# Gate and up products of four feed-forwards as seven block products each, in a two-block transformer kernel

## The reference, cut to what matters

```
x = x + 0.5 * swiglu(rms_norm(x, ffn_norm_g[l, 0]), ffn_w_gate[l, 0], ffn_w_up[l, 0], ffn_w_down[l, 0])
x = x + mixer(rms_norm(x, mix_norm_g[l]))
x = x + 0.5 * swiglu(rms_norm(x, ffn_norm_g[l, 1]), ffn_w_gate[l, 1], ffn_w_up[l, 1], ffn_w_down[l, 1])

swiglu(h, wg, wu, wd) = (silu(h @ wg) * (h @ wu)) @ wd      # wg, wu: 1024 x 2816, wd: 2816 x 1024
```

## Time and profile before

| | us |
|---|---|
| median of 3 runs | 3767.45 (3766.74 to 3774.5) |
| profiled execution, span from its first to its last instruction | 3773.9 |
| PE busy | 3591.6 (95%) |
| DVE, ACT, POOL busy | 1361.0, 1280.9, 1416.5 (36%, 34%, 38%) |

### The profile page before, as it was taken

One profiled execution on the slowest core, in us unless ns is written; L12 is line 12 of the kernel. 1 busy time (PEld: TensorE's weight loads), 2 busy tenths in 40 slices (PEclk: granted clock), 3 DMA queues, 4 the chain that ended last, 5 costly groups with the idle time before them and its releaser, 6 DMA issues. The chain is left out here.

```text
span 3773.9 us, 50732 instructions
## 1 busy us (share of the span) xinstructions
PE 3591.6 (95%) x18352; PEld 2848.7 (75%) x18352; DVE 1361.0 (36%) x1928; ACT 1280.9 (34%) x2014; POOL 1416.5 (38%) x756
## 2 busy tenths in 40 slices
PE   7999999999999999999999998999998997879998
PEld 6888776688887888666688886888886874648886
DVE  4233645542325223645542336111115104561112
ACT  4222435542224223435542224212123234243223
POOL 4444333344444444333344442223232430024443
PEclk8999999999999999999999999999998998889999
DMA  4332443233323333333233332222212321013331
GB/s 133 96 99 84 99 119 113 85 90 98 97 84 101 96 99 89 100 113 107 85 95 100 95 99 63 64 64 61 66 52 61 89 77 52 1 45 93 96 95 61
DMA packets 569026, 322.34 MB, mean 85 GB/s; under 512 B 30266, under 2 KB 563360, under 8 KB 568480
## 3 DMA queue, kind: packets, MB, share of 16 engines
q1 hardware_dynamic: 568864, 320.22, 29.1%
HBM read 318.08 MB, written 2.10 MB: 85 GB/s over the span
## 5 line engine op out<-in xcount | busy, mean ns | idle before, releaser
L874 POOL TENSOR_TENSOR w_lo<-w_raw,w_hi 128x1024 fp32r<-128x1024 f32 x516 | 1273.5, 2468 | 2109.4 <-ACT w_hi L919 2109.4
L919 ACT ACTIVATE w_hi<-w_raw 128x1024 fp32r<-128x1024 f32 x516 | 546.8, 1060 | 1800.7 <-PE psum L2163 1685.8
L2163 PE MATMUL psum<-xg_hi,w_hi 128*128 128x512 f32 x1456 | 572.7, 393 | 12.2 <-DVE xg_lo L1485 10.4
L2163 PE MATMUL psum<-xg_hi,w_lo 128*128 128x512 f32 x1456 | 568.2, 390 | 0.0
L2163 PE MATMUL psum<-xg_lo,w_hi 128*128 128x512 f32 x1408 | 549.5, 390 | 0.0
L2163 PE MATMUL psum<-h_hi,w_hi 128*128 128x512 f32 x1248 | 504.3, 404 | 30.7 <-DVE h_ctx_lo L1534 21.6
L2163 PE MATMUL psum<-h_lo,w_hi 128*128 128x512 f32 x1248 | 491.1, 394 | 0.0
L2163 PE MATMUL psum<-h_hi,w_lo 128*128 128x512 f32 x1248 | 491.1, 393 | 0.0
L2163 PE MATMUL psum<-a_hi,w_hi 128*128 128x512 f32 x1232 | 433.0, 375 | 4.9 <-DVE a_lo L1602 4.2
L2163 PE MATMUL psum<-a_lo,w_hi 128*128 128x512 f32 x1232 | 432.7, 374 | 0.0
L2163 PE MATMUL psum<-a_hi,w_lo 128*128 128x512 f32 x1232 | 432.3, 374 | 0.0
(11 more groups left out here) (454 smaller groups left out, 4399.7 us busy)
## 6 DMA issues: line engine op xcount, KB each, us to landing
w_raw<-ffn_w SPq DMA_DIRECT2D x120, 512.0 KB, 3.8
w_raw<-ffn_w_gate SPq DMA_DIRECT2D x88, 512.0 KB, 3.8
w_raw<-ffn_w_up SPq DMA_DIRECT2D x88, 512.0 KB, 3.8
ada_raw<-ada_w SPq DMA_DIRECT2D x72, 512.0 KB, 4.5
w_raw<-ffn_w_down SPq DMA_DIRECT2D x64, 512.0 KB, 4.1
w_raw<-w_in SPq DMA_DIRECT2D x60, 512.0 KB, 3.8
w_raw<-ffn_w_down SPq DMA_DIRECT2D x32, 384.0 KB, 3.4
w_raw<-w_out SPq DMA_DIRECT2D x24, 512.0 KB, 4.0
```

The costliest lines, as they stand in the source:

```text
L874: nc.gpsimd.tensor_tensor(w_lo[:, i, :], w_raw[:, i, :], w_hi[:, i, :].bitcast(F32), ALU.subtract).then_inc(lo_ready, 1)
L919: nc.scalar.activation(w_hi[:, pos, :], w_raw[:, pos, :], ACT.Copy).then_inc(hi_ready, 1)
L2163: last = nc.tensor.matmul(dst, w[:, pos, k * P:(k + 1) * P], rhs[g][r](k0 + k), start=k == 0 and m == 0, stop=k == nk - 1 and m == 2)
```

## The change

**The unit.** Gate and up of the four feed-forwards are no longer computed tile by tile. A *unit* is the gate (r = 0) or the up (r = 1) product for a pair of tiles, so 256 hidden features, 1024 inputs and 512 tokens. Weights and activations are cut into 2 x 2 blocks: hidden features by halves of the inputs (4 chunks each), halves of the inputs by halves of the tokens (256 each). The four blocks of the result come out of 7 block products instead of 8, by a scheme of the Strassen and Winograd kind. Each block product is 4 chunks x 3 passes = 12 matmuls of 256 tokens, so a unit has 84 matmuls of 256 where it had 48 of 512. There are 22 units in a feed-forward. PE does the products in the order 0, 2, 3, 1, 4, 6, 5. Products 0, 3, 4 and 5 accumulate into one bank (`chain`), and partial results are taken out of it between them.

**What feeds it.** The weights need 3 sums of 512 columns and a fourth one later (`set_sums_of`, `set_last_sum`), on DVE. The sums' rounded copies and rests come from ACT (`set_high`, `set_last_high`) and DVE (`sums_low`, `set_last_low`), and POOL makes two rests of 1024 per unit (`set_low`), as many as before. From a part's second pair on, two of the sums lie in PSUM, where ACT first copies a half slot (`copy_second`); a part's first pair has them in SBUF. The activations need 4 such sums, made once per feed-forward at its entry, chunk by chunk (`b_low` on DVE, `b_high` on ACT) in place of `xg_low` and `xg_high`.

**What follows it.** ACT copies three partial results per unit out of PSUM (`part_copy`), and DVE adds three and scales (`joined`). Silu, `a_hi` and `a_lo` are done once per pair on 1024 columns.

**Around it.** The loop over the two layers is written out. After F4 nothing is made for a next feed-forward (7 of `xg_high` and `xg_low` go), the load of `ctx_rows` starts later, and a Silu of the second block's conditioning has moved into the mixer. Counters of the second block are merged with those of the first.

The core of the diff (indentation shortened):

```diff
@@ GpSimd @@
+def set_low(turn, g, r):
+    hi, lo = set_hi[r], set_lo[r]
+    pool.wait_ge(*set_hi_ready(*g(3, 1)))
+    nc.gpsimd.tensor_tensor(lo[:, 0:SLOT], w_raw[:, 2 * r, :], hi[:, 0:SLOT].bitcast(F32), ALU.subtract).then_inc(set_lo_ready.sem, 1)
+    pool.wait_ge(*set_hi_ready(*g(3, 3)))
+    pool.wait_ge(*last_lo_ready(*g(1, 1)))
+    nc.gpsimd.tensor_tensor(lo[:, 2 * SLOT:3 * SLOT], w_raw[:, 2 * r + 1, :], hi[:, 2 * SLOT:3 * SLOT].bitcast(F32),
+                            ALU.subtract).then_inc(lo_ready, 2)
...
@@ ScalarE @@
+def b_high(layer, j, y, c, gain):
...
+    else:
+        i = c - HALF_K
+        nc.scalar.activation(b2_hi[:, i, :], x_lat[:, c, :], ACT.Identity, scale=gain(c)).then_inc(b_hi_ready.sem, 1)
+        for n, (hi, of) in enumerate(((t2_hi, t_keep), (t3_hi, b_keep), (t4_hi, t_keep))):
+            act.wait_ge(*b_sum(layer, j * B_SUMS + 2 * HALF_K + 3 * i + n + 1))
+            nc.scalar.activation(hi[:, i, :], of[:, i, :], ACT.Copy).then_inc(b_hi_ready.sem, 1)
+def copy_second(turn, r):
+    act.wait_ge(slot_loaded[2 * r + 1], turn * 16 + 16)
+    nc.scalar.activation(psum[:, 6, :], w_raw[:, 2 * r + 1, 0:SLOT // 2], ACT.Copy).then_inc(second_copied.sem, 1)
...
+def part_copy(g, r, out, n):
+    bank, dst = ((0, out[:, 0, 0:HALF_T]), (1, out[:, 1, HALF_T:T]), (0, out[:, 0, HALF_T:T]))[n]
+    act.wait_ge(*product_done(*g(6, n + 1)))
+    nc.scalar.activation(dst, psum[:, 3 * r + bank, 0:HALF_T], ACT.Copy).then_inc(parted.sem, 1)
...
+            set_high(turn, up, 1, steps=(0,))
+            part_copy(gate, 0, silu, 0)
+            set_high(turn, up, 1, steps=(2,))
+            part_copy(gate, 0, silu, 1)
+            part_copy(gate, 0, silu, 2)
+            if q == 0:
+                first()
+            set_high(turn, up, 1, steps=(1,), sums=later)
+            if q > pairs[0]:
+                a_high(q - 1)
+            set_last_high(up, 1)
+            turn += 1
+            if q < pairs[-1]:
+                if q == pairs[0]:
+                    act.wait_ge(*x_updated(layer, FFN_Y0[j] + part * KD))
+                else:
+                    act.wait_ge(*sums_lo_ready(*up(1, 1)))
+                copy_second(turn, 0)
+                set_high(turn, next_gate, 0, steps=(0,))
+            else:
+                down_high(turn, 0)
...
+            part_copy(up, 1, gated_1, 1)
+            part_copy(up, 1, gated_1, 2)
+            if q < pairs[-1]:
+                set_high(turn, next_gate, 0, steps=(1,), sums=sums)
+            act.wait_ge(*scaled(layer, j * (NF // 2) + q + 1))
+            nc.scalar.activation(silu[:], silu[:], ACT.Silu).then_inc(silu_done.sem, 2)
+            if q < pairs[-1]:
+                set_last_high(next_gate, 0)
+                act.wait_ge(*sums_lo_ready(*next_gate(1, 1)))
+                copy_second(turn, 1)
...
@@ VectorE: entry, sums of weights @@
+def b_low(layer, j, y, c, gain):
...
+    else:
+        i = c - HALF_K
...
+        nc.vector.scalar_tensor_tensor(t, second, g, t, ALU.mult, ALU.add).then_inc(b_sum.sem, 1)
+        nc.vector.scalar_tensor_tensor(keep, second, g, keep, ALU.mult, ALU.subtract).then_inc(b_sum.sem, 1)
+        dve.wait_ge(*b_hi_ready(layer, b0 + 1))
+        nc.vector.scalar_tensor_tensor(b2_lo[:, i, :], x_lat[:, c, :], g, b2_hi[:, i, :].bitcast(F32), ALU.mult, ALU.subtract).then_inc(b_lo_ready.sem, 1)
+        dve.wait_ge(*b_hi_ready(layer, b0 + 2))
+        nc.vector.tensor_tensor(t2_lo[:, i, :], t, t2_hi[:, i, :].bitcast(F32), ALU.subtract).then_inc(b_lo_ready.sem, 1)
+        nc.vector.scalar_tensor_tensor(t, first, g, t, ALU.mult, ALU.subtract).then_inc(b_sum.sem, 1)
+        dve.wait_ge(*b_hi_ready(layer, b0 + 3))
+        nc.vector.tensor_tensor(t3_lo[:, i, :], keep, t3_hi[:, i, :].bitcast(F32), ALU.subtract).then_inc(b_lo_ready.sem, 1)
+        dve.wait_ge(*b_hi_ready(layer, b0 + 4))
+        nc.vector.tensor_tensor(t4_lo[:, i, :], t, t4_hi[:, i, :].bitcast(F32), ALU.subtract).then_inc(b_lo_ready.sem, 1)
...
+def set_sums_of(turn, g, r, copied=None):
...
+        dve.wait_ge(*second_copied(*copied))
+        nc.vector.tensor_tensor(second[:, 0:half], first[:, 0:half], psum[:, 6, :], ALU.subtract).then_inc(set_sum.sem, 1)
+        nc.vector.scalar_tensor_tensor(psum[:, 6, :], psum[:, 6, :], -1.0, second[:, half:SLOT], ALU.mult, ALU.subtract).then_inc(set_sum.sem, 1)
+        dve.wait_ge(*set_sum(*g(4, 2)))
+        nc.vector.scalar_tensor_tensor(psum[:, 7, :], psum[:, 6, :], -1.0, first[:, 0:half], ALU.mult, ALU.subtract).then_inc(set_sum.sem, 1)
+def sums_low(g, r, copied=False, highs=3):
...
+    dve.wait_ge(*set_hi_ready(*g(3, highs)))
+    nc.vector.tensor_tensor(set_lo[r][:, at].rearrange("p (a n) -> p a n", a=2), psum[:, 6:8, :] if copied else set_sums,
+                            set_hi[r][:, at].bitcast(F32).rearrange("p (a n) -> p a n", a=2), ALU.subtract).then_inc(sums_lo_ready.sem, 1)
+def set_last_sum(g, r, copied=False):
...
+    dve.wait_ge(*set_lo_ready(*g(1, 1)))
+    dve.wait_ge(*set_sum(*g(4, 3)))
+    nc.vector.tensor_tensor(last, last, psum[:, 7, :] if copied else set_sums[:, 1, :], ALU.subtract).then_inc(set_sum.sem, 1)
+def set_last_low(turn, g, r):
+    dve.wait_ge(hi_ready, turn * SLOTS + (2 * r + 2))
+    nc.vector.tensor_tensor(set_lo[r][:, 3 * SLOT:SET], w_raw[:, 2 * r, SLOT // 2:SLOT], set_hi[r][:, 3 * SLOT:SET].bitcast(F32),
+                            ALU.subtract).then_inc(last_lo_ready.sem, 1)
...
@@ VectorE: a unit @@
+    def joined(turn, g, r, out, factor, between, done):
+        chain, w_part, whole = (psum[:, 3 * r + n, 0:HALF_T] for n in range(3))
...
+        dve.wait_ge(*product_done(*g(6, 4)))
+        dve.wait_ge(*parted(*g(3, 1)))
+        nc.vector.tensor_tensor(out_11, whole, out_11, ALU.add).then_inc(combined.sem, 1)
+        between(0)
+        dve.wait_ge(*product_done(*g(6, 5)))
+        dve.wait_ge(*parted(*g(3, 2)))
+        nc.vector.tensor_tensor(out_22, chain, out_22, ALU.add).then_inc(combined.sem, 1)
+        between(1)
+        dve.wait_ge(*product_done(*g(6, 6)))
+        dve.wait_ge(*parted(*g(3, 3)))
+        nc.vector.tensor_tensor(out_12, w_part, out_12, ALU.add).then_inc(combined.sem, 1)
+        dve.wait_ge(*combined(*g(3, 3)))
+        nc.vector.tensor_tensor(out[:, 0, :], out[:, 0, :], factor[0], ALU.mult)
+        nc.vector.tensor_tensor(out_22, out_22, factor[1][:, HALF_T:T], ALU.mult)
+        between(2)
+        dve.wait_ge(slot_used, turn * SLOTS + (SLOTS + 2 * r + 2))
+        nc.vector.tensor_tensor(out_21, chain, factor[1][:, 0:HALF_T], ALU.mult).then_inc(*done)
...
-            for i in range(2):
...
-                dve.wait_ge(slot_used, (turn + it) * SLOTS + (SLOTS + 2 * i + 1))
-                nc.vector.tensor_tensor(silu_1[:, i, :], psum[:, 3 * i, :], rstd[:, 0:T], ALU.mult).then_inc(scaled.sem, 1)
...
+            def during_gate(at):
+                if at == 0:
+                    sums_low(up, 1, later)
+                if at == 1:
+                    set_last_sum(up, 1, later)
+                    if q == 0:
+                        inverse_root(layer, v, [(0, T)], 7)
+                    if later:
+                        a_low(q - 1)
+                if at == 2:
+                    set_last_low(turn, up, 1)
...
+            def during_up(at):
+                if at == 0 and not last:
+                    sums_low(next_gate, 0, True)
+                if at == 1:
+                    if not last:
+                        set_last_sum(next_gate, 0, True)
+                    dve.wait_ge(*silu_done(layer, f + 2 * q + 2))
+                    nc.vector.tensor_tensor(silu[:], silu[:], rstd[:, 0:T].rearrange("p (o n) -> p o n", o=1).broadcast_to([P, 2, T]),
+                                            ALU.mult).then_inc(rooted.sem, 1)
+                    dve.wait_ge(*rooted(layer, j * (NF // 2) + q + 1))
+                if at == 2 and not last:
+                    set_last_low(turn + 1, next_gate, 0)
...
@@ TensorE @@
-    def gate_and_up(turn, tile, i, first=False):
-        pe.wait_ge(*gated_ready(layer, tile - 1))
-        for u in range(2):
-            pe.wait_ge(lo_ready, turn * SLOTS + (SLOTS + 2 * i + u + 1))
-            dense(2 * i + u, 0, KD, [xg], [psum[:, 3 * i + u, :]], rows_ready(layer, v + 1 if v else 0) if first and u == 0 else None).then_inc(slot_used, 1)
...
+def product(r, block, dst, hi, lo, cols, onto=False, before=None):
+    for k in range(HALF_K):
+        if before is not None:
+            before(k)
+        at = slice(block * (SLOT // 2) + k * P, block * (SLOT // 2) + (k + 1) * P)
+        for m, (w, x) in enumerate(((set_hi, hi), (set_hi, lo), (set_lo, hi))):
+            last = nc.tensor.matmul(dst, w[r][:, at], x[:, k, cols], start=not onto and k == 0 and m == 0, stop=k == HALF_K - 1 and m == 2,
+                                    skip_group_check=True)
+    return last
+def late_ffn(layer, j, v, s, f, y):
+    def unit(turn, r, g, tile, first=False):
```

(24 more changed lines are left out.)

512 lines of the change are left out of this document (341 added, 171 removed).

## The result

The changed kernel takes 3782.74 us by the median of 20 runs, the kernel before 3770.35 in the same comparison; the ratio is 1.0026, with a 95% interval of 1.0015 to 1.0038. It is slower by 0.26%, where 0.4% faster was forecast.

A forecast was written before the change was run, and what follows sets the result against it. TensorE's matmul pace was taken to bound the kernel. Units -68.9, their losses +3, entries +50, and +4, -3, -1.5 gave -16.4: a median of about 3751, stated as 3752 us, 8 in 10 for 3727 to 3790.

The forecast's parts named there:

- A: Steady units of the four feed-forwards: 10.06 us per unit against 10.88 per tile, 84 units, -68.9 us.
- the slack at product 5: Inside a unit, product 5 waits for VectorE's L1852; about 1 us was thought to remain before it is late.
- C: The rest: part starts +4, `a_lo` waits -3, work dropped after F4 -1.5, loop written out and counters 0.
- Eight parts start behind a down product with SBUF sums beside POOL: 0.5 each, +4: Part starts within the feed-forwards: sums with SBUF operands beside GpSimd cost +4 us in all, range 0 to 12.
- B: The four feed-forward entries: F1 +16, F2 and F4 +10.5 each, F3 +13, together +50 us, believed 30 to 66.
- The `a_lo` waits, 4 x 1.0, go: -3: TensorE's four waits for `a_lo`, 1.0 us each, taken to lie inside the tiles, would disappear: -3 us.
- E: End of TensorE's last matmul before a feed-forward's entry, from which the entry's steps were counted.
- a collision of 1.4: F2's and F4's entries: a VectorE instruction with both operands in SBUF held until GpSimd is done, about 1.4 us.
- inside the ends: Entries: first products after the wait at 0.21 us per matmul were left to the entries' ranges.
- two collisions: F3's entry: two VectorE instructions held beside GpSimd raise its cost from +10.6 to +13 us.
- A loop over two layers written out ... 0: Loop over the layers: written out, it issues the same work and costs or gains 0 us.
- Rival 2: Entries cost more, VectorE's queue being hit beside GpSimd: 74 us in all, +7.6, 3775 us; chance 0.22.

The follow-up runs named there:

- the experiment through PSUM: Changed kernel with the first pair's up weight sums of each feed-forward's second and third parts formed through PSUM: 3762.91 us, ratio 0.9969 to the kernel before.
- two more edits: Added to the changed kernel with part-start sums through PSUM: root after the sums' rounded copy (3757.98 us), then the entries' first-pair sums through PSUM too (3753.72 us).

## Why the prediction was wrong

**A held.** The pitch of 0.120, 10.08 per unit and hardly a wait inside later units are as worked out; the slack at product 5 was enough. By the rule of the Trainium skill ("TensorE: Matmul & The Clock Gate", section "Wait — 56ns, not 53.3ns?") a unit would have been 9.17, an estimate; the trace has 10.08.

**C failed, and took the gain.** The step that failed is "Eight parts start behind a down product with SBUF sums beside POOL: 0.5 each, +4". By TensorE's matmuls a part start costs 2.1 against the steady pace, 16.6 for the eight, and the experiment through PSUM gives 2.0 each back. With 0.5 each the changed stretches would have come out some 7 us faster than before instead of 6 slower. Against the forecast of -16.4, B's miss alone would have left -10, this one together with the next none of the gain. The mechanism was in the text, and the rows of 2.9 us could have been had from it: GpSimd's second rest of one set and its first of the next stand back to back, so two DVE instructions in a row with both operands in SBUF are held, each to the end of one of them. The groups of the changed kernel:

```profile
L1701 DVE TENSOR_TENSOR w_raw<-w_raw 128x512 f32<-128x512 f32 x24 | 60.4, 2516 | 0.0
...
L1703 DVE SCALAR_TENSOR_TENSOR set_sums<-set_sums,w_raw 128x512 f32<-128x512 f32 x24 | 40.3, 1680 | 0.0
```

Against 0.69 that is 44 and 24 us of VectorE's time. The exclusive lock of the Trainium skill ("SBUF — State Buffer", section "Who interferes with whom") was cited rightly, the trace agrees (2.9 beside GpSimd, 0.69 otherwise), and the prediction priced it too low.

A second term of C failed: "The `a_lo` waits, 4 x 1.0, go: -3". No reason was given for it. The four waits are not inside the tiles, as the prediction has it, but in each feed-forward's last down product, and there they stayed, 5.0 us after 4.2. That is 4 us more. None of the prediction's own signs of being wrong (units above 10.3 us, entries outside 30 to 66) watched either term, and none of them came.

**B was short by 6 us.** In F2 the order was right: the part copy that I put at E + 13.1 stands at 810.66, 13.4 behind E (797.2). TensorE's own waits in F2's entry, for product 2 and product 3, and the first matmul of product 5:

```profile
805.58 0.58 PE L2548 MATMUL psum<-t_hi,set_hi 128*128 128x256 f32 x1 [6.75 <-DVE set_lo L1715]
...
811.07 0.58 PE L2548 MATMUL psum<-t_hi,set_hi 128*128 128x256 f32 x1 [2.56 <-ACT silu L1024]
...
819.59 0.39 PE L2548 MATMUL psum<-t_hi,set_hi 128*128 128x256 f32 x1
```

Its last matmul of the unit ends at 821.1, E + 23.9, where the sum had 22.2 and a collision of 1.4, so 23.6. The collision was there, but it is not what the time went to. VectorE and then ScalarE:

```profile
811.13 2.87 DVE L1701 TENSOR_TENSOR w_raw<-w_raw 128x512 f32<-128x512 f32 x1
...
813.92 2.87 DVE L1703 SCALAR_TENSOR_TENSOR set_sums<-set_sums,w_raw 128x512 f32<-128x512 f32 x1
...
817.97 1.23 DVE L1715 TENSOR_TENSOR set_lo<-set_sums,set_hi 128x1024 fp32r<-128x1024 f32 x1 [0.69 <-ACT set_hi L1014]
819.11 0.42 DVE L1852 TENSOR_TENSOR silu<-psum,silu 128x256 f32<-128x256 f32 x1
```

```profile
810.66 0.36 ACT L1024 ACTIVATE silu<-psum 128x256 f32<-128x256 f32 x1
...
814.09 1.06 ACT L1018 ACTIVATE set_hi<-w_raw 128x1024 fp32r<-128x1024 f32 x1 [3.07 <-DVE w_raw L1701]
```

Both sums stand 2.2 us too long and ScalarE waits 3.07 for the first, yet L1852 is done when product 5 is due, and TensorE doesn't wait again in this unit. What it lost behind product 3's start is the clock:

```profile
804.00:808.00 4.00, 2.42 (x11) 2.42 (x12) 4.00 (x8) 2.04 (x4) 0.00 (x0) 0.50 0.01 2
808.00:812.00 4.00, 1.44 (x7) 1.15 (x7) 3.76 (x7) 2.67 (x5) 1.25 (x1) 0.50 0.00 0
```

TensorE waited 6.8 and 2.6 us there, and the granted clock was 0.50, the lower level (1.2 GHz), so products 2 and 3 ran at 0.21 a matmul, 2.6 us each instead of 1.44. The prediction expected this rate, but put it "inside the ends" and not into the sum. In F1 and F3 product 5 did wait for L1852, 1.2 and 0.7 us.

F3's entry was the one most in error, 33.3 us from E (1159.7) to TensorE's last matmul of the unit, where the sum and two collisions give 31.1. VectorE's backlog was as forecast up to the addition of chunk 7 to `x_lat` (1169.65 with 0.68, so 10.6 behind E; forecast 10.7). Then L1682 stood 2.57 us beside GpSimd, and the part copy started at 1180.90, 21.2 behind E, some 2 us late.

**"A loop over two layers written out ... 0" was wrong by 5 us.** It didn't enter the sum's error, since F3's entry was counted from F2's last matmul. It means that the block products themselves cost 5 us more against a kernel without the seam: in the same comparison the changed kernel again (3784.6) stood 20 us above the kernel before with its loop written out (3764.73).

**Rival 2 came closest by its number**, +7.6 by 74 us of entries, but its place was wrong. The hits on `b_low` came as it had them: 16 of its instructions (L1670, L1672, L1674, L1681, L1682) were held beside GpSimd, five each in F2, F3 and F4, 28 us of VectorE's time. But all but one of these fifteen come while TensorE still works on the product before E, and the entries came to 56, not 74. The hits that TensorE had to wait for are mostly those on the weights' sums, at the part starts. The result lies in the stated range, and slower had a chance of 0.24.

**What stays open.** The changed stretches show +5.8 and +5.4 us, the medians +12.4 and +7.5, the ratios 0.26% and 0.20%. The difference lies in stretches with unchanged code that take one of a few values per execution, and in F1 of the one profile of before. Whether the changed program takes the slow values more often can't be told from two profiles. Why the clock rose 8 us earlier in one of two equal entries stays open too.

## What to carry to other kernels

A scheme that saves TensorE work has to be priced at its entries and seams, not in its steady state: 84 units gained 67 us on TensorE, and 12 places, the four entries and eight part starts, lost 73. Take the ends of such places at TensorE's own matmuls: VectorE's last instruction of a unit stood 2.4 us behind TensorE at an entry, where the kernel before had 0.3, and so the entries seemed to cost 7 us more than they did. Before SBUF-to-SBUF work is given to VectorE beside a busy GpSimd, look whether GpSimd's instructions stand back to back there; moving one operand to PSUM took 2.9 us down to 0.7, and brought the kernel level with the one before with its loop written out; it took two more edits to get 16 us below that. Write out a long loop that is entered twice when a chain crosses its end, and run the written-out kernel alone, or its gain is credited to something else, here 5 us of what looked like the block products'.
